# A two-layer mixer kernel: query weights loaded a stage earlier, another order for the first tile's norm, range clears, and four stores moved from GpSimd to SyncE

## The reference, cut to what matters

```python
for l in range(2):
    m_lat = split(silu(c) @ w_ada[l] + b_ada[l], 6)           # and m_ctx from c_ctx
    u = modulate(h, m[0], m[1])                               # norm without weights, scale, shift
    pa, pb, pc, pd = split(u @ w_in[l])
    ya = diff_attention(pa); yd = neighbourhood_attention(pd)
    yb = rwkv7(pb)                                            # chunked scan, both directions
    yc = gated_deltanet(pc)                                   # chunked scan, both directions
    mix = concat(ya, yb, yc, yd) @ w_out[l]
    h = post_norm(h, m[2], mix, ln_mix_g[l], ln_mix_b[l])
    t = modulate(h, m[3], m[4])
    q = (t @ w_q).reshape(heads=8, 2, 128)                    # w_q is in_peer_wq, 1024 x 2048
    s = einsum('thpd,hpnd->thpn', q, keys)                    # 128 keys a half
    # the best 16 of each half, the best 16 of their 256 sums: 128 rows per token
    ffn = sum_k gate_k * gelu(t . u_k) * v_k
    h = post_norm(h, m[5], ffn, ln_ffn_g[l], ln_ffn_b[l])
```

## Time and profile before

| | us |
|---|---|
| median of three runs | 5723.88 |
| the runs | 5714.44, 5723.88, 5766.38 |
| time of the profiled execution | 5718.22 |
| its span, first to last instruction | 5715.5 |
| PE busy | 4691.0 (82%) |
| DVE busy | 3512.9 (61%) |
| ACT busy | 1967.5 (34%) |
| POOL busy | 1754.0 (31%) |

### The profile page before, as it was taken

The page is one execution under the profiler, slowest core; times in us unless marked ns, Lnnn a source line. Parts: engine busy times, 40 slices in busy tenths (PEclk is TensorE's granted clock), DMA queues, the critical chain, the costliest instruction groups (busy, mean ns, idle before and its releaser), DMA issues. The chain is left out here.

```text
span 5715.5 us, 93413 instructions
## 1 busy us (share of the span) xinstructions
PE 4691.0 (82%) x35878; PEld 2643.9 (46%) x35878; DVE 3512.9 (61%) x7609; ACT 1967.5 (34%) x5447; POOL 1754.0 (31%) x1775
## 2 busy tenths in 40 slices
PE   7988799768888797978877698779976878888777
PEld 3555599543334242524322255459954434334222
DVE  2675544377867677676764457554437786867644
ACT  1333333113333433434333223343311434333333
POOL 0110032004544444444443202103211454444432
PEclk8997899889999999999999899879988999999999
DMA  8756412429999999999999886302243999999998
GB/s 293 265 186 227 184 57 67 166 71 421 421 421 420 420 414 421 415 421 415 414 421 421 330 286 237 122 31 81 56 166 131 421 421 421 419 421 415 421 421 345
DMA packets 385936, 1729.79 MB, mean 303 GB/s; under 512 B 86120, under 2 KB 158360, under 8 KB 217368
## 3 DMA queue, kind: packets, MB, share of 16 engines
q0 software_dynamic: 195840, 1384.89, 59.0%
q1 hardware_dynamic: 159880, 261.24, 13.2%
q10 hardware_dynamic: 29776, 77.70, 3.7%
HBM read 1640.75 MB, written 86.65 MB: 302 GB/s over the span
## 5 line engine op out<-in xcount | busy, mean ns | idle before, releaser
L2410 PE MATMUL pe_ps<-pe_ring,pe_diag 128*128 128x512 f32 x5120 | 2450.8, 613 | 616.6 <-ACT pe_diag L2444 610.2
L2478 DVE SCALAR_TENSOR_TENSOR pe_ring<-pe_ring,ro_tb 128x1024 f32<-128x1024 f32 x1280 | 1562.1, 1225 | 941.9 <-DMA pe_ring<-in_peer_uv,ro_slot 922.6
L2055 POOL DMA_INDIRECT pe_ring<-in_peer_uv,ro_slot x1280 | 1430.5, 1118 | 2260.5 <-PE pe_ps L2410 1766.6
L2410 PEld LDWEIGHTS pe_ps<-pe_ring,pe_diag 128*128 128x128 f32 x5120 | 897.1, 190 | 2061.3 <-ACT pe_diag L2444 1341.2
L2438 ACT ACTIVATE pe_wts<-pe_raw 128x1 f32<-128x1 f32 x1280 | 258.5, 202 | 1751.6 <-DVE pe_ring L2478 1750.4
L922 PE MATMUL pp_ps<-pp_win,pp_uT 128*128 128x439 f32 (+6 forms) x1728 | 597.7, 505 | 10.4 <-issue 8.7
L2444 ACT ACTIVATE pe_diag<-c_ident,pe_wts 128x128 f32<-128x128 f32 x1280 | 513.9, 401 | 42.0
L922 PEld LDWEIGHTS pp_ps<-pp_win,pp_uT 128*128 128x128 f32 x1728 | 326.4, 195 | 266.9 <-issue 175.4
L2440 ACT ACTIVATE pe_wts<-pe_wts,ro_gates 128x1 f32<-128x1 f32 x1280 | 376.5, 294 | 41.6
L1360 POOL TENSOR_TENSOR ch_m<-ch_at,ch_joins 128x256 f32<-128x256 f32 x288 | 204.0, 747 | 464.3 <-DVE ch_at L1659 464.3
L2113 PEld LDWEIGHTS pe_ps<-ro_tbT,peer_wq 128*128 128x128 f32 x2048 | 248.8, 192 | 61.2 <-issue 61.2
(11 more groups left out here) (358 smaller groups left out, 5171.6 us busy)
## 6 DMA issues: line engine op xcount, KB each, us to landing
pp_win<-in_w_in SPq DMA_DIRECT2D x24, 1756.0 KB, 10.7
at_aw<-in_w_ada SPq DMA_DIRECT2D x10, 4096.0 KB, 13.3
gd_dram<-pp_gout POOLq DMA_DIRECT2D x48, 448.0 KB, 7.9
pe_ring<-in_peer_uv,ro_slot POOLq DMA_INDIRECT x1280, 15.1
ch_nat<-gd_dram SPq DMA_DIRECT2D x44, 448.0 KB, 4.0
peer_wq<-in_peer_wq ACTq DMA_DIRECT2D x2, 8192.0 KB, 30.0
rw_dram<-pp_out POOLq DMA_DIRECT2D x48, 320.0 KB, 5.2
ch_nat<-rw_dram SPq DMA_DIRECT2D x48, 320.0 KB, 4.2
```

Source lines behind the costliest of these rows:

```text
L2055: return pool.indirect_dma_start(dst, None, table, bass.IndirectOffsetOnAxis(ap=index, axis=0))
L2410: mm = pe.matmul(ps[:, y_bank(p) + c, :], diag[:, n % DIAGS, :], ring[:, n % RING, D + c * 512:D + (c + 1) * 512], start=(k == 0), stop=(k ...
L2478: v.scalar_tensor_tensor(row, row, 1.0, tb[p % 2][:], ALU.mult, ALU.mult, accum_out=raw[p % 2][:, k:k + 1]).then_inc(dots_done, 1)
```

## The change

Five edits:

1. `stage` clears semaphores by ranges of consecutive numbers, one instruction for each range.
2. In the inflow, the last tile's four stores from `gout` are issued by SP, with a semaphore of their own, and POOL's last wait counts four stores fewer.
3. `wq` is allocated ahead of the chunk stage and loaded in it by SP in four parts of 2 MB, after the stores of chunks 5, 7, 9 and 11. PE's wait and ACT's DMA in the outflow go; SP waits for the parts at the end of the chunk stage.
4. To make room, the chunk stage's six difference tiles become two, `near_dd` and `all_dd`, written in place. DVE waits for its own first result before it overwrites `all_dd`.
5. In the outflow, DVE, ACT and SP take tile 0's norm and route norm ahead of tiles 2 and 3; `keys` and `iota` are loaded ahead of tile 1's `h` and tile 2's rows.

```diff
@@ stage
+        numbers = sorted(s.num for s in sems)
+        starts = [k for k in range(len(numbers)) if k == 0 or numbers[k] != numbers[k - 1] + 1]
+        together = [range(numbers[a], numbers[b - 1] + 1) for a, b in zip(starts, starts[1:] + [len(numbers)])]
...
-                    for s in sems:
-                        pool.sem_clear(s)
+                    for numbered in together:
+                        pool.sem_clear(numbered)
...
@@ inflow_stage, sync
+                sp.wait_ge(gout_ready, TILES)
+                store_chunks(sp, last_stored, s["gd"], gout, TILES - 1, (TILES + 3) % TILES + CTX_TILES)
+                sp.wait_ge(last_stored, 64)
                 for i in range(TILES):
                     sp.wait_ge(tile_gone, i + 1)
@@ inflow_stage, gpsimd
-                    pool.wait_ge(gout_ready, i + 1)
-                    store_chunks(s["gd"], gout, i, back)
-                    pool.wait_ge(stored, 16 * 16 * (i + 1))
+                    if i + 1 < TILES:
+                        pool.wait_ge(gout_ready, i + 1)
+                        store_chunks(pool, stored, s["gd"], gout, i, back)
+                    pool.wait_ge(stored, 16 * (16 * (i + 1) - (0 if i + 1 < TILES else 4)))
@@ chunk_stage
+WQ_AT = (5, 7, 9, 11)
...
                     store(c)
                     if c + SLOTS_IN < CHUNKS:
                         load(c + SLOTS_IN)
+                    if c in WQ_AT:
+                        part = WQ_AT.index(c)
+                        sp.dma_start(wq[:, 2 * part:2 * part + 2], t["peer_wq"][l].rearrange("(k p) n -> p k n", p=P)[:, 2 * part:2 * part + 2]).then_inc(wq_in, 16)
+                sp.wait_ge(wq_in, 16 * len(WQ_AT))
...
-                    if c:
-                        act.wait_ge(at1_ready, c)
-                        act.wait_ge(ddm_ready, c)
-                    act.activation(dd_a[:], du_a[:], ACT.Exp, scale=-1.0).then_inc(dd_ready, 1)
+                    act.activation(near_dd[:], near_dd[:], ACT.Exp, scale=-1.0).then_inc(dd_ready, 1)
...
+                    if c:
+                        v.wait_ge(g_kept, 2 * c - 1)
+                    v.tensor_tensor(all_dd[:], ps[:, A_BANKS[1], 0], gc(c), ALU.subtract).then_inc(raw_ready, 1)
                     v.wait_ge(raw_ready, c + 1)
                     if c:
-                        v.wait_ge(dd_ready, 2 * c)
-                    v.tensor_scalar(du_a[:], raw[:], 0.0, None, ALU.max).then_inc(du_ready, 1)
-                    v.tensor_scalar(du[:], raw[:], 0.0, None, ALU.min).then_inc(du_ready, 1)
+                        v.wait_ge(at1_ready, c)
+                    v.tensor_scalar(near_dd[:], all_dd[:], 0.0, None, ALU.max).then_inc(du_ready, 1)
+                    v.wait_ge(du_ready, 2 * c + 1)
+                    v.tensor_scalar(all_dd[:], all_dd[:], 0.0, None, ALU.min).then_inc(du_ready, 1)
@@ outflow_stage, sync
+                for dst, src in ((b["keys"][:], t["keys"][l]), (b["iota"][:], t["k_iota"])):
+                    sp.dma_start(dst, src).then_inc(keys_in, 16)
                 load_h(1)
                 load_y(2)
-                for dst, src in ((b["keys"][:], t["keys"][l]), (b["iota"][:], t["k_iota"])):
-                    sp.dma_start(dst, src).then_inc(keys_in, 16)
@@ outflow_stage, scalar
-                act.dma_start(wq[:], t["peer_wq"][l].rearrange("(k p) n -> p k n", p=P)).then_inc(wq_in, 16)
                 turned_y(1)
-                po_roots(2)
                 z_root(0)
                 route_root(act, r, 0)
                 for n in range(2):
                     route_turned(act, r, 0, n)
+                po_roots(2)
+                z_root(1)
                 po_roots(3)
-                z_root(1)
@@ outflow_stage, vector
                 po_last(1)
-                po_first(2)
                 post_first(0)
                 post_last(0)
                 v.wait_ge(z_ready, 1)
                 route_norm_first(v, link, r, 0)
+                route_norm_last(v, link, r, 0)
+                po_first(2)
                 po_last(2)
-                route_norm_last(v, link, r, 0)
+                post_first(1)
+                post_last(1)
                 po_first(3)
-                post_first(1)
                 po_last(3)
-                post_last(1)
                 route_steps(0, 8)
@@ route_query
-        if p == 0:
-            pe.wait_ge(r["wq_in"], 16)
@@ build
-            chunk_stage(nc, l, t, s, consts)
             with sbuf(nc, l, "peer_wq", [P, KT, PH * 2 * P]) as wq, ExitStack() as kept:
+                chunk_stage(nc, l, t, s, wq, consts)
```

More of the change, by code:

```diff
@@ L133, in _ @@
                 def _(sp):
-                    for s in sems:
-                        sp.sem_clear(s)
+                    for numbered in together:
+                        sp.sem_clear(numbered)
 def sbuf(nc, l, name, shape, dt=F32):
@@ L818, in inflow_stage, with store_chunks @@
              f_ready, low_ready, low_done, lowT_ready, raw_done, raw_ready, gates_ready, g_copied, sums_done, ex_ready, exps_ready,
-             sq_ready, root_ready, dve_step, out_ready, stored, abs_ready, exp_ready, g_ready, gsums_done, conv_ready, qkv_ready,
+             sq_ready, root_ready, dve_step, out_ready, stored, last_stored, abs_ready, exp_ready, g_ready, gsums_done, conv_ready, qkv_ready,
              gate_ready, beta_ready, gsq_ready, groot_ready, dec_ready, gexps_ready, gout_ready) = sems
             h_in, w_in, gone = (h0_in, h1_in), (w0_in, w1_in), (gone0, gone1, gone2)
+            def store_chunks(eng, landed, dst, src, i, back):
+                for d, tile in ((0, i), (1, back)):
+                    for half in range(2):
+                        eng.dma_start(dst[tile, half, d].rearrange("b t q a e -> t b (q a e)"),
+                                      src[half * C:(half + 1) * C, d].rearrange("t b q a e -> t b (q a e)")).then_inc(landed, 16)
             @block.sync
@@ L875, in _ @@
                 pool.memset(a2[:], 0.0).then_inc(zeroed, 1)
[L877 to L882, removed]
                 for i in range(TILES):
@@ L896, in _ @@
                     pool.wait_ge(out_ready, i + 1)
-                    store_chunks(s["rw"], out, i, back)
+                    store_chunks(pool, stored, s["rw"], out, i, back)
                     pool.dma_start(s["rwpost"][i], post[:, i % 2]).then_inc(stored, 16)
-                    pool.wait_ge(gout_ready, i + 1)
-                    store_chunks(s["gd"], gout, i, back)
-                    pool.wait_ge(stored, 16 * 16 * (i + 1))
+                    if i + 1 < TILES:
+                        pool.wait_ge(gout_ready, i + 1)
+                        store_chunks(pool, stored, s["gd"], gout, i, back)
+                    pool.wait_ge(stored, 16 * (16 * (i + 1) - (0 if i + 1 < TILES else 4)))
                     pool.sem_inc(tile_gone, 1)
@@ L1254, in chunk_stage @@
         rkb = [sb(f"rkb{u}", [P, 2, N4, C]) for u in range(3)]
-        diag, raw, du, du_a, dd, dd_a, ddm = [sb(n, [P, N4, C]) for n in ("diag", "raw", "du", "du_a", "dd", "dd_a", "ddm")]
+        diag, near_dd, all_dd = [sb(n, [P, N4, C]) for n in ("diag", "near_dd", "all_dd")]
         dec1 = [sb(f"dec1_{u}", [P, N4]) for u in range(3)]
@@ L1570, in decays @@
                     act.wait_ge(du_ready, 2 * c + 1)
[L1571 to L1574 removed]
+                    act.activation(near_dd[:], near_dd[:], ACT.Exp, scale=-1.0).then_inc(dd_ready, 1)
                     act.wait_ge(du_ready, 2 * c + 2)
[L1576 removed]
+                    act.activation(all_dd[:], all_dd[:], ACT.Exp).then_inc(dd_ready, 1)
                 def keep_right(c):
@@ L1664, in near_decayed @@
                     v.wait_ge(dd_ready, 2 * c + 2)
-                    v.tensor_tensor(by_pair(ddm[:]), by_pair(dd[:]), over_pairs(near[:, 1]), ALU.mult).then_inc(ddm_ready, 1)
+                    v.tensor_tensor(by_pair(all_dd[:]), by_pair(all_dd[:]), over_pairs(near[:, 1]), ALU.mult).then_inc(ddm_ready, 1)
                 def mask_first(c):
```

21 lines of the change are left out of this document (10 added, 11 removed).

## The result

The changed kernel takes 5681.22 us (median of 20 runs, 5667.12 to 5730.71); the kernel before took 5719.97 us beside it (median of 20, 5708.27 to 5766.38). The ratio is 0.994, with an interval of 0.9924 to 0.9956. The forecast was 5645 us, range 5622 to 5672: the sign is right, the gain is 38.8 us instead of 75.5, and the median lies above the range. The profiled execution took 5667.12 us, span 5665.2, which is 50.3 us less than the span before; it was the shortest of the twenty, so this text goes by the stages of the profiled executions and not by their sums.

A forecast was written before the change was run, and what follows sets the result against it. It took waits in stages closed by barriers to bound the kernel, chiefly PE's outflow waits for the route's input. Gains of 52.1 + 27.8 + 8.2 less 12.6 make 75.5 us; from 5721 it forecast 5645 us, range 5622 to 5672.

The forecast's parts named there:

- Everything there hangs on PE, and moves with it: Outflow, layer 0: work after the query groups, including DVE's later 18.05 us wait, moves earlier with PE, so the gain lasts.
- The faster first group of the forecast: Outflow: first query group takes 7.31 us instead of 9.11 and 9.85, gaining 1.8 and 2.5 us.
- the 52.1 forecast: Outflow, both layers: PE's waits for the route's input go and the first query groups quicken, 52.1 us gained.
- The parts after chunks 5, 7 and 9 are hidden: Chunk stage: these weight loads cost nothing, some 8 us each against 26.6 us iterations and slots three iterations ahead.
- The slower rival: Chunk stage: weight parts on SP's queue hold PE up, 15 us each, 90 us in all, giving 5735 us; chance 0.02.
- PE's idle time in the chunk stage grows: Chunk stage: one of the signs named in advance that would show the prediction wrong.
- The last part: Chunk stage's end: the weights after chunk 11 are exposed behind the last stores, costing 6.3 us a layer, 12.6 in all.
- Clears: Stage ends: one range clear in each of nine SP and four POOL stages replaces single clears, 27.8 us gained.
- The rival by which a range costs what its members cost: Stage ends: range clears gain nothing, the 27.8 us stay, giving 5673 us; chance 0.08.
- Last stores of the inflow: Inflow's end: with SP issuing the stores POOL drains earlier and ACT sets the end, 8.2 us gained.
- Tiles in place and keys: Chunk stage's added DVE waits and the outflow's loads of keys: nothing counted; rival of late keys, 5668 us, chance 0.06.

The follow-up runs named there:

- The new order: Changed kernel with ACT taking tile 3's root behind the first query group's copies instead of ahead of them; 5658.66 us, ratio 0.9877 to the kernel before.
- ranges alone: Kernel before with only the range clears on SP and POOL; 5693.14 us, ratio 0.9937 to the kernel before.
- the kernels with tiles in place and no parts: Changed kernel with ACT loading the query weights whole in the outflow again: 5666.34 us; also with tile 3's root behind the first query group: 5651.99 us.
- the two without: The kernel before, unchanged, 5719.97 us, and the kernel before with only the range clears, 5693.14 us.
- the doubled run: Changed kernel, tile 3's root behind the first query group, four weight parts after chunks 4, 6, 8, 10, each loaded twice; 5668.86 us, ratio 0.9896.
- parts early: Changed kernel, tile 3's root behind the first query group, four weight parts after chunks 4, 6, 8, 10 instead of 5, 7, 9, 11; 5650.03 us, ratio 0.9874.
- small parts: Changed kernel, tile 3's root behind the first query group, weights in eight 1 MB parts after chunks 3 to 10; 5649.82 us, ratio 0.9871.

## Why the prediction was wrong where it was wrong

**Outflow: the step that failed is "Everything there hangs on PE, and moves with it".** The prediction worked out when DVE has the route's input and when PE is free, and both came true. It then let the query groups follow on PE at their old pace. It did not read ACT's new order against the new times. The kernel before has the same root ahead of the same copy, and ACT's timeline of it shows why that cost nothing there:

```profile
1160.42 0.21 ACT L1901 ACTIVATE mx_rr<-mx_rr 128x8 f32<-128x8 f32 x1 [1.22 <-DVE mx_rr L1963]
...
1168.44 0.60 ACT L2156 ACTIVATE ro_qT<-mx_ps 128x512 f32<-128x512 f32 x1 [3.50 <-PE mx_ps L2113]
```

The root was taken 8.0 us before the copy, and the copy waited for PE. With the first query group 26 us earlier in the stage (1127.36 - 1071.8 against 1159.30 - 1077.9), and DVE's first half of tile 3 now behind the whole route input, the copy waits for the root. The price was 9.5 us a layer of idle time, 0.9 for the scores, and in layer 0 1.4 for the second query group, both at a lower granted clock. The faster first group of the forecast (7.38 us against 7.31) did come true. The new order gives 8.7 + 10.5 = 19.2 us back, with 2.1 us of the wait in layer 0 left. The rest of the step held: with that order mended, 26.4 + 27.1 = 53.5 us against the 52.1 forecast.

**Chunk stage: the step that failed is "The parts after chunks 5, 7 and 9 are hidden".** The prediction looked for a part in the way of the chunks' own loads, and saw three iterations of slack and a DMA share of 0.22. Both are true, and PE's waits for DMA in the stage did not grow (19.0 and 14.3 us before, 17.2 and 13.2 after). They say nothing of PE's own instructions, which come over the same DMA engines (last section). The six parts inside the pipeline cost 14.0 us, or 11.9 against kernels with tiles in place. The slower rival had the right place and the wrong mechanism, the loads and stores on SP's queue: it decided from 12.6 us a part, and a part costs about 2. The prediction had named "PE's idle time in the chunk stage grows" as what would prove it wrong, and that is what the issue waits show.

**The last part** was priced right: 6.3 us a layer forecast; the tail after is 11.7 and 12.2 against 5.6 and 5.7 without it, 12.6 us in all.

**Clears**: 27.8 forecast, 25.6 measured. The term took one range a stage at the price of one clear; there are 26 ranges, and a long one takes up to 0.3 us. The rival by which a range costs what its members cost is out.

**Last stores of the inflow**: 8.2 forecast. From ACT's last issue of `p_dram` to the barrier's end went 7.7 and 7.6 us with ranges alone, and 3.3 and 3.3 after: 8.7 us.

**Tiles in place and keys**: nothing was counted. DVE has no wait for the keys in the outflow, and the kernels with tiles in place and no parts take 374.8 and 367.4 us to PE's end in the mean, the two without 373.9 and 364.1. A cost of up to 3 us in layer 1 is inside the scatter and stays open; if it is there, it is part of the 14.0 us.

The sum now: 75.5 - 19.2 (ACT's order) - 14.0 (parts) - 2.2 (clears) + 0.5 (stores) + 1.4 (the rest of the outflow) = 42.0 us, against 38.8 between the medians. That they meet so closely is partly luck, since stages without an edit differ by more (below). That the sign held is not: the clears, the stores and the last part came out within 2.2 us each of what was forecast for them.

## What to carry to other kernels

When a stall of 24 us goes, read each in-order stream around it at its new times: an instruction that was harmless because its producer was long done can become the head of the queue for the very result that is now early. Put waits for later tiles behind the copies that feed the busiest engine. A low mean DMA share doesn't make a bulk load free beside an engine with a dense instruction stream; price it by the bytes, here 0.9 to 1.2 us a MB, and compare it with the place that it leaves. And a load that is waited for at a stage's end belongs ahead of the last store's wait.

## What the runs showed of the hardware that was not expected

**PE waits for its instructions while bulk data moves.** The page of the kernel after lists the DMA queues (packets, MB, share of the 16 engines' span), and two of them carry instructions:

```profile
q8 instruction: 288, 4.72, 0.3%
q14 instruction: 149, 1.22, 0.1%
```

Together 5.94 MB for the 93,013 instructions of the span, 64 bytes each, moved during the run and on the same 16 DMA engines as the weights. The Trainium skill, page "Trainium Architecture — The Big Picture", section "The software stack", has instructions of 64 bytes, with which this agrees, and says that the streams are moved into each engine's memory when the program is loaded; these rows show them moving while it runs, so here the measurement decides. In layer 0's chunk stage (391 us) PE runs 11,544 matmuls and as many weight loads, and queue q8 moves 91 packets of 16 KB, or 256 instructions, which fits these 23,088 instructions of PE.

The records of single packets show that PE's issue waits are waits for these packets. In the chunk stages of the ten profiled executions there are 155 such waits before PE's end. Every one of them ends 0.9 to 1.7 us after the end of a q8 packet, nine in ten 1.25 to 1.6 us after it; of moments drawn at random only a quarter lie 0.8 to 1.8 us behind one. That holds without weights too. What the parts change is when a packet moves, not for how long: a q8 packet takes about 1.0 us inside a part and outside. They start 3.8 us apart in the median, and in a part up to 6.7 and 7.2 us apart in layer 0 of the kernel after. Here are the two around the wait of 2.06 us that ends at 976.17. Three windows of the DMA queues (packets, MB, share of the 16 engines), 967.0 to 968.1, 968.1 to 973.7 and 973.7 to 974.7:

```profile
q8 instruction: 1, 0.02, 5.6%
...
q1 hardware_dynamic: 913, 2.02, 101.1%
...
q8 instruction: 1, 0.02, 5.8%
```

In the 5.6 us of the middle window no instruction packet moves and the data queue q1 fills all 16 engines; the second packet ends at 974.7, and PE goes on 1.5 us later. When a packet is asked for is not in the records, so that it stands behind the weights' data in the DMA engines' queues is argued and not shown. In the doubled run the issue waits are most of the growth in layer 0 (12.8 of 14.8 us) and less of it in layer 1 (10.7 of 17.5). In layer 1 the granted clock of that stage was 0.97 where the kernels without parts have 0.98 to 0.99; as an estimate, 1% of 366 us is some 4 us of the remainder. The rest has no row of its own.

**Scatter sits in the attention stages.** With no edit there, layer 1's attention stage took 177.5 to 179.0 us in eight of the ten executions profiled, 198.0 in one and 221.7 in another. The windows of that stage in the runs with parts early and with small parts, both in the new ACT order, show why: the same 778 matmuls, at a granted clock of 0.60 and of 0.82 (same columns as above):

```profile
3636.80:3858.50 221.70, 198.89 (x778) 135.11 (x778) 108.90 (x176) 76.71 (x165) 0.00 (x0) 0.60 0.07 24
```

```profile
3624.00:3802.00 178.00, 150.39 (x778) 103.24 (x778) 108.75 (x176) 76.88 (x165) 0.10 (x1) 0.82 0.08 30
```

Layer 0's attention stage went from 230.0 to 241.8 us in the same way. Differences of some 10 us between medians of five runs mean little here. Stages with the same code are sharper: the outflows with the same order and loads agree within 1.5 us, the chunk stage to PE's end within some 6.
